# Delta gates moved into the merged mixer stage, with nine attention steps ahead of the first delta head, and two column groups side by side behind a norm

## The chip, the cores and the metric

The kernel runs on one core of a Trainium2 chip. The metric is the device time of one execution in microseconds, the median of several. TensorE (PE in the rows, PEld for its weight loads), VectorE (DVE), ScalarE (ACT), GpSimd (POOL) and the DMA queue that SyncE (SP) issues on each work through their own list of instructions in order. They meet only at semaphores.

## What is computed

Two transformer blocks of two layers each, on 512 tokens of width 1024. The change touches the second block only. Each of its layers does this:

```python
h = rms_norm_2(x, pre_mix_w[l])
u = h @ w_in[l]
(u_conv, dq, dk, dv, gqkv, gz, b_f, b_b, a_f, a_b) = jnp.split(u, offs, axis=-1)
y_conv = conv_module(u_conv, ...)
y_diff = diff_attention(dq, dk, dv, ...)
y_delta = gated_deltanet(gqkv, gz, b_f, b_b, a_f, a_b, ...)
y = jnp.concatenate([y_conv, y_diff, y_delta], axis=-1) @ w_out[l]
x = x + rms_norm_2(y, post_mix_w[l])
h = rms_norm_2(x, pre_mlp_w[l])
y = jnp.square(jax.nn.relu(h @ w_ff1[l])) @ w_ff2[l]
x = x + rms_norm_2(y, post_mlp_w[l])
```

`diff_attention`: six heads; for each block of 128 queries, two softmax maps over 512 keys with a slope times distance, the second subtracted with a factor lambda, then the product with the values. `gated_deltanet`: six heads of width 64, forward and backward. Its gates are `g = -exp(A_log) * softplus(a + dt_bias)` and `beta = sigmoid(b)`; in each chunk a unit lower triangular system is solved, and a state runs from chunk to chunk.

## The kernel before

The layer runs as a sequence of stages. Each has one block of instructions for every engine, and the engines meet at its end.

**Gate stage** (`delta_gates_stage`, L2598). TensorE turns the 24 gate rows (L2615) and six tiles of keys and values to token order (L2620, 24 transposes), then sums the log decays (L2626, L2628). ACT computes the sigmoid, exponentials and logarithm; DVE copies the turned tiles out (L2654).

**Mixer stage** (`mixer_stage`, L2682). It merges the differential attention (24 steps, one for each of six heads and four query blocks) with the delta heads. The delta work of a head stands in seven slots, levels 0 to 6 of the triangular solve; the program counts slots `t = 7 h + level`. In a slot TensorE does `turn(…, 0)` (L2804), `pairs` (L2792 or, at level 0, L2794), `turn(…, 1)`, work of the head before (`before`), an attention piece, `products` (L2812), the preparation of the next head and more of the head before (`behind`), and a second attention piece. ACT copies the turned halves (L2996) and the pairs (L3000); DVE subtracts the products (`update`, L3251), which lets the next level begin. Slots 42 to 48 hold only the states of the last head and the last attention steps.

**An attention step** `s` runs over four to five slots. Lag 0: TensorE's scoring, `scores` (L2899 the slope times distance, L2906 the query-key products). Lag 1: DVE's maximum (`top`, L3190), ACT's exponentials (`exps`, L3019). Lag 2: DVE's inverses, ACT's `rescale` (L3025), DVE's `subtract` (L3204). Lag 3: TensorE turns the first half of the map, ACT copies it (L3031), TensorE turns the second (L2918). Lag 4: ACT copies, TensorE weighs the values (`weigh`, L2925), ACT copies the output (L3036). Steps start every second slot. The scores of all steps share banks 5 and 6, and the numbers come from one line:

```python
s, odd = divmod(t + 2 - lag, 2)
```

Ahead of slot 0 stand the values' transposes (L2942), the first head's preparation (`prepare(0, …)`: two transposed rows of gate sums, L2777, then the key and the query Gram products, L2779) and the scoring of step 0 alone.

**Dense products** (class `Dense`, `run`). Columns are taken in groups of 256. Weights of a unit are split into two halves, high by ACT (L254), low by DVE (L259), in two slots, and TensorE runs low, high by low, high by high (L460 to L462) for each of eight row tiles. Where a `PlainNorm` with `post` goes ahead (`ff1_0`, `in2_1`, `ff1_1`), it first scales the last product by its own norm (L1247), adds it to the stream (L1251 on DVE, L1266 on GpSimd for tiles 1, 3, 5), splits the new stream tile (L1214 on ACT, L1230 on DVE), squares it (L1219), and TensorE sums the squares (L1008) behind each tile of group 0. ACT and DVE split the weights of group 1 when the norm is through. The second norm's factor is spread (L1016) behind tile 3 of group 1, DVE copies it (L1164), and the results are multiplied by it at evacuation (L688, or L675 in `in2_1`).

## Time and profile before

| what | value |
|---|---|
| median of 3 runs | 4175.57 us (4174.79 to 4177.26) |
| the profiled execution | 4178.55 us, span 4176.8 us |
| granted TensorE clock, mean | 0.944 of full |
| PE busy / DVE / ACT / POOL | 3872.8 / 2183.3 / 1495.6 / 344.1 us |
| gates, layers 0 and 1 | from 2418 and from 3381 us |
| `ff1_0`, `in2_1`, `ff1_1` norms | from 2802, 3191 and 3765 us |

All times inside the trace are from the span's start. A granted clock of 0.50 is 1.2 GHz, 1.00 is 2.4 GHz. In rows that list instructions in order of time, "x8" is eight of a kind merged, and the bracket is the idle time of the engine just before and what ended it. A matmul in float32 stands as two passes in the trace, so `weigh` has eight.

### The profile page before, as it was taken

What the parts mean: (1) busy time and instruction counts of PE and PEld (TensorE: products, weight loads), DVE (VectorE), ACT (ScalarE), POOL (GpSimd) and SP (SyncE); (2) the same over time, 40 slices, a digit from 0 to 9 for tenths busy, and PEclk for the clock granted to TensorE, in tenths of its full rate; (3) what the DMA queues carried; (4) which work ended last, traced back from release to release, by engine and by line L of the source; (5) the groups of instructions that cost most, each with busy time, mean ns of one, the idle gap of its engine ahead of it and who ended that gap; (6) DMA issues with size and microseconds to landing.
All of it is one profiled execution on the core that took longest, in us unless ns stands there. A gap on an engine that the chain in (4) does not pass through costs nothing. (4 is left out here: it accounts for less than half of the span.)

```text
span 4176.8 us, 49727 instructions
## 1 busy us (share of the span) xinstructions
PE 3872.8 (93%) x20585; PEld 3106.2 (74%) x20585; DVE 2183.3 (52%) x3124; ACT 1495.6 (36%) x2290; POOL 344.1 (8%) x296
## 2 busy tenths in 40 slices
PE   7997789999999999899999979989998979988998
PEld 4884667888888777678877757757786757866876
DVE  5625765555564332373256746543475846544375
ACT  2115632111453112152255335433364335533264
POOL 0000220000000000000000034200000025400000
PEclk9998889999999999999999979989999979989998
DMA  5500013343222111122322100022231200012231
GB/s 202 174 31 10 6 41 101 111 141 111 66 66 74 58 58 51 38 91 91 100 83 94 61 11 1 1 71 81 90 101 61 87 11 1 1 61 71 91 101 60
DMA packets 254720, 288.90 MB, mean 69 GB/s; under 512 B 6756, under 2 KB 226939, under 8 KB 254517
## 3 DMA queue, kind: packets, MB, share of 16 engines
q1 hardware_dynamic: 252437, 281.84, 20.8%
q10 hardware_dynamic: 2080, 4.19, 0.3%
q8 instruction: 146, 2.39, 0.2%
q14 instruction: 57, 0.47, 0.0%
HBM read 283.92 MB, written 2.10 MB: 68 GB/s over the span
## 5 line engine op out<-in xcount | busy, mean ns | idle before, releaser
L460 PE MATMUL banks<-h_halves,w_halves 128*128 128x512 f32 x3824 | 1435.4, 375 | 83.1 <-DVE h_halves L259 42.3
L461 PE MATMUL banks<-h_halves,w_halves 128*128 128x512 f32 x3824 | 1427.5, 373 | 0.0
L462 PE MATMUL banks<-h_halves,w_halves 128*128 128x512 f32 x3824 | 1420.8, 372 | 0.0
L460 PEld LDWEIGHTS banks<-h_halves,w_halves 128*128 128x128 f32 x3824 | 733.6, 192 | 233.1 <-issue 84.2
L462 PEld LDWEIGHTS banks<-h_halves,w_halves 128*128 128x128 f32 x3824 | 731.0, 191 | 128.0
L461 PEld LDWEIGHTS banks<-h_halves,w_halves 128*128 128x128 f32 x3824 | 733.5, 192 | 121.1 <-issue 0.5
L259 DVE TENSOR_TENSOR w_halves<-work,w_halves 128x2048 fp32r<-128x2048 f32 (+1 forms) x215 | 488.4, 2271 | 469.3 <-ACT w_halves L254 469.1
L254 ACT ACTIVATE w_halves<-work 128x2048 fp32r<-128x2048 f32 (+1 forms) x215 | 407.4, 1895 | 533.7 <-PE banks L462 399.6
L254 ACT ACTIVATE h_halves<-kept 128x512 fp32r<-128x512 f32 (+1 forms) x520 | 333.0, 667 | 313.8 <-PE banks L462 234.4
L259 DVE TENSOR_TENSOR h_halves<-kept,h_halves 128x512 fp32r<-128x512 f32 (+1 forms) x520 | 361.3, 738 | 138.6 <-ACT h_halves L254 137.9
L952 DVE SCALAR_TENSOR_TENSOR kept<-kept 128x512 f32<-128x512 f32 x280 | 188.3, 748 | 7.1 <-DMA kept<-in_mod_w 7.1
L694 ACT ACTIVATE kept<-kept 128x512 f32<-128x512 f32 x64 | 37.4, 633 | 253.8 <-DVE kept L688 253.8
L2119 PE MATMUL banks<-h_halves,w_halves 128*128 128x512 f32 x320 | 121.4, 379 | 3.7 <-DVE h_halves L1116 3.7
L2120 PE MATMUL banks<-h_halves,w_halves 128*128 128x512 f32 x320 | 118.9, 372 | 0.0
L2121 PE MATMUL banks<-h_halves,w_halves 128*128 128x512 f32 x320 | 118.4, 370 | 0.0
L709 ACT ACTIVATE kept<-banks 128x512 f32<-128x512 f32 x66 | 30.0, 529 | 245.9 <-PE banks L462 245.9
L3119 POOL TENSOR_TENSOR work<-work 128x512 f32<-128x512 f32 x84 | 108.9, 1301 | 70.2 <-PE banks L2792 52.4
L3251 DVE TENSOR_TENSOR work<-work,banks 128x512 f32<-128x512 f32 x84 | 62.5, 745 | 94.6 <-PE banks L2812 94.6
L688 DVE SCALAR_TENSOR_TENSOR kept<-banks,kept 128x512 f32<-128x512 f32 x64 | 41.2, 686 | 135.4 <-PE banks L462 135.3
L2135 PE MATMUL banks<-w_halves,h_halves 128*128 128x256 f32 x384 | 108.7, 283 | 0.0
L2134 PE MATMUL banks<-w_halves,h_halves 128*128 128x256 f32 x384 | 108.7, 283 | 0.0
L2133 PE MATMUL banks<-w_halves,h_halves 128*128 128x256 f32 x384 | 108.7, 283 | 0.0
(366 smaller groups left out, 4576.7 us busy)
## 6 DMA issues: line engine op xcount, KB each, us to landing
work<-in_w_ff SPq DMA_DIRECT2D x64, 1024.0 KB, 5.3
work<-in_ffn_w_in SPq DMA_DIRECT2D x44, 1024.0 KB, 5.1
kept<-in_mod_w SPq DMA_DIRECT2D x40, 1024.0 KB, 5.2
work<-in_odd_w_in SPq DMA_DIRECT2D x24, 1024.0 KB, 5.2
work<-in_w_in SPq DMA_DIRECT2D x24, 1024.0 KB, 5.0
work<-in_ffn_w_out SPq DMA_DIRECT2D x16, 1024.0 KB, 5.2
work<-in_even_w_in SPq DMA_DIRECT2D x13, 1024.0 KB, 5.1
work<-in_odd_w_out SPq DMA_DIRECT2D x8, 1024.0 KB, 5.4
```

Source lines behind the costliest of these rows:

```text
L254: return core.nc.scalar.activation(dst, src, ACT.Copy)
L259: return core.nc.vector.tensor_tensor(dst, src, high.bitcast(F32), ALU.subtract)
L460: nc.tensor.matmul(o, low[:, k - a, fc], rh[:, tc], start=(k == 0), stop=False)
L461: nc.tensor.matmul(o, high[:, k - a, fc], rl[:, tc], start=False, stop=False)
L462: mm = nc.tensor.matmul(o, high[:, k - a, fc], rh[:, tc], start=False, stop=(k == K - 1))
L952: ins = nc.vector.scalar_tensor_tensor(out=self.sum(q, n), in0=self.slot(m)[:, k], scalar=c, in1=self.sum(q, n), op0=ALU.mult, op1=ALU.add)
L2119: nc.tensor.matmul(o, low[:, c, fc], rh, start=(c == 0), stop=False)
L2120: nc.tensor.matmul(o, high[:, c, fc], rl, start=False, stop=False)
L2121: mm = nc.tensor.matmul(o, high[:, c, fc], rh, start=False, stop=(c == KD - 1))
L2133: nc.tensor.matmul(o, core.h(c, 1)[:, tc], high[:, c, :], start=(c == 0), stop=False)
L2134: nc.tensor.matmul(o, core.h(c)[:, tc], low[:, c, :], start=False, stop=False)
L3119: nc.gpsimd.tensor_tensor(c4(pl.level[m % 3]), c4(pl.s[h % 2]), mat(pl.pairs[:, cc(lv)]), ALU.mult).then_inc(level_masked, 1)
```

## The change

**Gates in the mixer stage.** `delta_gates_stage` is gone. Its transposes, sums and activations are spread over the head of `mixer_stage`: gate rows into bank 2, token tiles alternately into banks 3 and 4. The loads are issued in another order: gate rows and the distance table first, the level masks (`pairs`) last.

**Nine attention steps ahead of slot 0.** Ten iterations, numbered -10 to -1, run before the level loop (called iterations 0 to 9 below). Steps 0 to 8 start in them, one each in iterations 0 to 8, with their scores alternately in banks 5, 6 and 0, 1. Token transposes stand in iterations 0 to 2, the four preparations of head 0 in iterations 3 to 6. The other 15 steps start 2.75 slots apart. Within a slot the weighing now stands ahead of the turn.

```diff
-    score_bank = lambda m: core.ps[:, 5 + m, :]
+    score_banks = lambda s: (0, 2) if s < AHEAD and s % 2 else (5, 7)
+    score_bank = lambda s, m: core.ps[:, score_banks(s)[0] + m, :]
...
+    AHEAD, EARLY = 9, 10
...
+    starts = {t: s for s, t in enumerate([s - EARLY for s in range(AHEAD)] +
+                                         [1 + (11 * i + 2) // 4 for i in range(N - AHEAD)])}
+
     def step_at(t, lag):
-
-        s, odd = divmod(t + 2 - lag, 2)
-        return s if odd == 0 and 0 <= s < N else None
+        return starts.get(t - lag)
...
+            for t in range(-EARLY, 0):
+                n = t + EARLY
+                if step_at(t, 4) is not None:
+                    weigh(step_at(t, 4))
+                if step_at(t, 0) is not None:
+                    scores(step_at(t, 0))
+                if n < 3:
+                    if n == 2:
+                        gate_totals()
+                    for b in range(2 * n, 2 * n + 2):
+                        tokens(b)
+                if step_at(t, 3) is not None:
+                    turn_step(step_at(t, 3), 0)
+                if 3 <= n < 7:
+                    prepare(0, n - 3)
+                if step_at(t, 3) is not None:
+                    turn_step(step_at(t, 3), 1)
```

That was TensorE's list; these are ACT's and DVE's:

```diff
+            for t in range(-EARLY, 0):
+                n = t + EARLY
+                if step_at(t, 4) is not None:
+                    copy(step_at(t, 4), 1)
+                if step_at(t, 2) is not None:
+                    rescale(step_at(t, 2))
+                if step_at(t, 4) is not None:
+                    out(step_at(t, 4))
...
+                if 3 <= n < 6:
+                    prepare(0, n - 3)
+                if step_at(t, 1) is not None:
+                    exps(step_at(t, 1))
+                    if step_at(t, 1) in split_at:
+                        split(split_at[step_at(t, 1)])
+                if step_at(t, 3) is not None:
+                    copy(step_at(t, 3), 0)
...
+                if step_at(t, 2) is not None:
+                    invert(step_at(t, 2))
+                if step_at(t, 1) is not None:
+                    top(step_at(t, 1))
...
+                if n in (3, 4):
+                    differences(0, n - 3)
+                    low(0, n - 3)
+                    exponents(0, n - 3)
+                    queries(0, n - 3)
+                if n == 5:
+                    key_gram(0)
+                if n == 6:
+                    query_gram(0)
+                if step_at(t, 2) is not None:
+                    subtract(step_at(t, 2))
```

The pairs of slot 0 wait until all nine early steps have left banks 0 and 1 (`pe.wait_ge(exped, 2 * AHEAD)`).

**Two groups side by side.** Where the norm has `post`, tile `k` of group 0 is followed by tile `k - 2` of group 1. Group 1's weights are split ahead of the norm's tiles, and the second norm's factor is spread behind both groups. The weights of group 2 are then split ahead of the evacuation of group 0.

```diff
                 if before is not None:
-                    second(eng)
+                    second(eng, (lambda: weights(0, 1)) if paired else None)
...
+                    if paired and isinstance(i, int) and i * B * C + u == 0:
+                        weights(i, u + 2)
+                        evacuate(i, u)
...
+                def two_groups():
+                    lag = before.LAG
+                    for k in range(K + lag):
+                        if k < K:
+                            group_tile(0, k)
+                            before.after_tile(pe, 0, k)
+                        if k >= lag:
+                            group_tile(1, k - lag)
+                    before.behind_groups(pe)
```

The order of instructions shows it at three places. TensorE at the start of the gates, before: the gate rows (L2615) and tokens, the gate sums, then the values of the attention (L2942), and one scoring (L2899, L2906) among the preparations (L2777, L2779).

```order
L2615 MATMUL banks<-kept 128x24 x4
L2620 MATMUL banks<-kept 128x128 x24
L2626 MATMUL banks<-work 128x24 x2
L2628 MATMUL banks<-work,kept 128x48
L2603 UNCONDITIONAL_BRANCH
L2761 UNCONDITIONAL_BRANCH
L2942 MATMUL banks<-kept 128x128 x12
L2777 MATMUL banks<-kept,work 128x128 x4
L2899 MATMUL banks<-work 128x512 x2
L2906 MATMUL banks<-p_halves 128x512 x6
```

After, at the same place (L2944 the values, L2881 and L2888 the scoring, L2926 the tokens, L2934 and L2936 the gate sums):

```order
L2940 MATMUL banks<-kept 128x24 x4
L2944 MATMUL banks<-kept 128x128 x12
L2881 MATMUL banks<-work 128x512 x2
L2888 MATMUL banks<-p_halves 128x512 x6
L2926 MATMUL banks<-kept 128x128 x8
```

The first scoring has moved up to directly behind the values; the 24 token transposes stand in three lots of eight behind the first three scorings.

TensorE in iteration 4 of the new order: weighing (L2907), scoring, first turn (L2900), a row preparation (L2755), second turn.

```order
L2907 MATMUL banks<-work,kept 64x128 x4
L2881 MATMUL banks<-work 128x512 x2
L2888 MATMUL banks<-p_halves 128x512 x6
L2900 MATMUL banks<-kept 128x128 x2
L2755 MATMUL banks<-kept,work 128x128 x4
L2900 MATMUL banks<-kept 128x128 x2
```

Before, the second row preparation stood between the first scoring and the Gram products, with no other step in flight.

```order
L2906 MATMUL banks<-p_halves 128x512 x6
L2777 MATMUL banks<-kept,work 128x128 x4
L2779 MATMUL banks<-kept 128x128 x8
L2794 MATMUL banks<-kept,work 128x128 x4
L2899 MATMUL banks<-work 128x512 x2
```

Each row preparation now stands inside an attention iteration, ahead of the turn that ends it.

ACT at the head of a paired norm, before (L1026 loads the root's table, L1021 the root, L1214 the high part of a stream tile, L1219 its square):

```order
L507 UNCONDITIONAL_BRANCH
L1026 ACTIVATE kept<-kept 128x1
L1021 ACTIVATE kept<-banks,kept 4x128
L1214 ACTIVATE h_halves<-stream,kept 128x512
L1219 ACTIVATE stream<-stream 128x2x256
```

and after, with the weights of group 1 (L254) between the root and the first tile:

```order
L545 UNCONDITIONAL_BRANCH
L1064 ACTIVATE kept<-kept 128x1
L1059 ACTIVATE kept<-banks,kept 4x128
L254 ACTIVATE w_halves<-work 128x2048
L1259 ACTIVATE h_halves<-stream,kept 128x512
L1264 ACTIVATE stream<-stream 128x2x256
```

L254 stood behind the norm's last root before.

## Rows read from the trace of the kernel before

**Rows 1.** Stretches: PE, PEld, DVE, ACT, POOL busy (count), granted clock, DMA.

```profile
3395.00:3423.20 28.20, 12.89 (x49) 9.34 (x50) 14.41 (x26) 5.65 (x12) 18.27 (x17) 0.56 0.07 19
...
3503.70:3546.00 42.30, 40.36 (x319) 32.96 (x317) 27.11 (x60) 21.53 (x53) 19.50 (x19) 1.00 0.01 1
3546.00:3586.60 40.60, 38.47 (x305) 32.39 (x305) 24.72 (x57) 22.04 (x54) 18.31 (x17) 1.00 0.00 1
...
3663.90:3697.00 33.10, 27.41 (x137) 17.66 (x136) 10.79 (x34) 13.58 (x33) 0.00 (x0) 0.74 0.11 35
```

**Rows 2.** Instructions in time: start, length in us, engine, line, idle before.

```profile
3380.81 0.39 PE L2615 MATMUL banks<-kept 24*128 24x24 f32 x4 [1.65 <-PEq L415]
...
3402.25 1.47 POOL L3123 CAST work<-kept 128x896 f16<-128x896 f32 x1 [191.56 <-DMA work<-in_diff_lambda_k]
...
3404.36 1.01 PE L2899 MATMUL banks<-work 128*128 128x512 f16 x2 [5.70 <-POOL work L3074]
...
3409.40 2.08 PE L2779 MATMUL banks<-kept 64*128 64x128 f32 x8 [1.41 <-DVE work L3210]
...
3422.86 1.03 PE L2899 MATMUL banks<-work 128*128 128x512 f16 x2 [5.07 <-ACT kept L3019]
3423.82 1.64 PE L2906 MATMUL banks<-p_halves 32*128 32x512 f32 x6
3425.39 1.11 PE L2804 MATMUL banks<-kept,work 128*128 128x128 f32 x4
```

**Rows 3.** DMA view, 3380 to 3402: issues, KB each, median us to landing.

```profile
kept<-tables SPq DMA_DIRECT2D x1, 448.0 KB, 3.1
```

**Rows 4.** Instructions in time: the parts of an attention step.

```profile
3421.35 0.69 ACT L3019 ACTIVATE kept<-banks,kept 128x512 f32<-128x512 f32 x1 [1.75 <-DVE kept L3192]
...
3439.98 0.38 PE L2918 MATMUL banks<-kept 128*128 128x128 f32 x2
...
3444.59 1.09 PE L2925 MATMUL banks<-work,kept 128*64 128x128 f32 x8
...
3447.78 0.60 PE L2899 MATMUL banks<-work 128*128 128x512 f16 x2
3448.32 0.97 PE L2906 MATMUL banks<-p_halves 32*128 32x512 f32 x6
```

**Rows 5.** Groups by line: the level update; busy us, mean ns, idle before.

```profile
L3251 DVE TENSOR_TENSOR work<-work,banks 128x512 f32<-128x512 f32 x84 | 62.5, 745 | 94.6 <-PE banks L2812 94.6
```

**Rows 6.** Instructions in time: the stage's end, after the last level update.

```profile
3664.63 0.66 PE L2835 MATMUL banks<-work 128*128 128x64 f32 x4 [0.56 <-DVE work L3251]
...
3670.88 0.66 PE L2835 MATMUL banks<-work 128*128 128x64 f32 x4 [0.20 <-DVE work L3259]
...
3688.84 1.97 PE L2925 MATMUL banks<-work,kept 128*64 128x128 f32 x8 [0.47 <-ACT work L3031]
...
3691.89 2.19 ACT L1440 ACTIVATE work<-kept 128x512 f32<-128x512 f32 x4 [0.28 <-PEq L2754]
```

**Rows 7.** Instructions in time: norm and first two groups of `ff1_1`.

```profile
3770.49 0.75 DVE L1247 SCALAR_TENSOR_TENSOR kept<-kept,banks 128x512 f32<-128x512 f32 x1 [2.17 <-PE banks L1016]
...
3774.66 0.76 PE L460 MATMUL banks<-h_halves,w_halves 128*128 128x512 f32 x1 [4.21 <-DVE h_halves L1230]
...
3784.19 1.04 PE L1008 MATMUL banks<-stream,kept 128*4 128x128 f32 x8
...
3798.57 2.29 DVE L259 TENSOR_TENSOR w_halves<-work,w_halves 128x2048 fp32r<-128x2048 f32 x1 [0.86 <-ACT w_halves L254]
...
3801.01 0.47 PE L460 MATMUL banks<-h_halves,w_halves 128*128 128x512 f32 x1 [4.67 <-DVE w_halves L259]
...
3809.53 0.69 DVE L1164 COPY kept<-banks 128x512 f32<-128x512 f32 x1 [8.67 <-PE banks L1016]
...
3816.49 0.47 PE L460 MATMUL banks<-h_halves,w_halves 128*128 128x512 f32 x1 [1.41 <-DVE w_halves L259]
```

**Rows 8.** Stretches, columns as in rows 1: 4 us of the tail.

```profile
3672.00:3676.00 4.00, 4.00 (x22) 2.57 (x19) 1.19 (x3) 0.27 (x1) 0.00 (x0) 0.57 0.02 4
```

344 lines of the change are left out of this document (199 added, 145 removed).

## The prediction

> **What bounds the kernel now.** I read the stretches of the second delta layer first (its stage of 317 us occurs once for each of the two layers, and nearly the same). In a stretch of the level loop TensorE is busy 40.36 of 42.30 us with four attention scorings in it, and 38.47 of 40.60 us with three [rows 1]: 1.7 us less time for 1.9 us less work. There TensorE is the bound and a moved attention step gives back its TensorE work. Before and behind that loop it is not. From 3395.0 to 3423.2 it is busy 12.89 us and its granted clock is 0.56, that is, nearly all at 1.2 GHz; behind the last level update it is busy 27.41 of 33.10 us at 0.74 [rows 1]. Then I read the instructions in order of time. The first scoring waits 5.70 us for GpSimd's slope, the second 5.07 us for the first step's exponentials [rows 2]. Last I read the norm ahead of the dense products: TensorE stands 4.67 us before the second group of columns, because ACT and DVE split that group's weights only when the norm is done [rows 7].
>
> **Part 1: gates merged, nine steps ahead of the loop.** My mark is the first turning matmul of level 1, at 3425.4 [rows 2]; in the new order it follows iteration 9 and one slot.
>
> Start. The table behind the scoring takes 3.1 us to land [rows 3]. It is now the third load, issued some 1 us into the stage, and the cast no longer waits for the lambda rows. Cast to scoring took 2.1 us (3402.25 to 3404.36) [rows 2]. With the first transposes of the gates at 3380.8 [rows 2] the first scoring comes at about 3381.9 + 3.3 + 2.4 = 3387.6, against 3404.4. So the gates' own stretch goes.
>
> Prices. At the low clock a scoring is 2.53 us (3422.86 to 3425.39) [rows 2], a weighing 1.97 [rows 6], a turn about 0.65 (twice less its drain: 0.38 at full clock) [rows 4], a preparation of four transposes 1.1 and of a Gram product 2.08 [rows 2]. At the full clock: 1.44 for the scoring (0.60 and 0.97 overlapping), 1.09, 0.38, and half of the others [rows 4]. The exponentials take ACT 1.5 us (3421.35 to the scoring at 3422.86 that waits for them) [rows 2, 4]; the two copies, the rescale and the output copy about 1.7 more.
>
> An iteration is a ring over ACT and TensorE: copy 0.4, weighing 1.1, output copy 0.3, exponentials 1.5, copy 0.4, turn 0.5: 4.2 us at the full clock. At the low clock TensorE sets it: copy 0.4, weighing 1.97, scoring 2.53, turn, copy and turn 1.7: 6.6 us. The three iterations with a row preparation are longer, since ACT reads the prepared rows ahead of its exponentials in program order, and DVE makes its differences ahead of the next subtraction. Walked through with these prices: iterations 0 to 2 (scoring, key and value transposes, gates) 3387.6 to 3402.4; iteration 3, 7.5 us; iteration 4, with weighing, scoring, turn, preparation, then 3.7 us of ACT and a turn in a row, 10.3; iteration 5, 8.2, to 3428.4. In it TensorE has no gap. In the kernel before it had none from 3422.86 on, at the low clock, and by 3439.98 the turns run at full clock [rows 2, 4]. So iterations 6 to 9 run mostly at full clock: 5.2, 5.9 (the query Gram product stands ahead of a subtraction), 4.3, 4.1, to 3448; slot 0 with pairs, weighing and two turns 3.0 to 3.5. The mark comes at about 3451.5: **+26 us** in each layer. Bounds: +15 if the clock is full all the way, +35 if it stays low.
>
> Level loop. Slots 1 to 41 lose 5 scorings, 6 turns in pairs and 4 weighings: 5 x 1.4 + 6 x 0.7 + 4 x 1.0 = 15.2 us. But the steps now stand every 2.75 slots, and eight slots hold no attention at all. A level is a ring: turns, pairs, ACT's copy, products, and DVE's 0.745 us update [rows 5]. Its two holes (some 0.65 us until the copy, an estimate, and 0.8 until the update) are filled today by attention; I count 6 us of holes left open, nearly half of them in head 0 and the rest at levels 6 and 0. Net **-9 us**; bounds -13 and -4. The slots just behind the mark ran at the low clock until about 3430; if half of that goes, **-1**.
>
> Tail. From the first value product at 3664.63 to the next stage's first instruction at 3691.89 [rows 6] the last head's four chunk steps share TensorE with two scorings, three turnings and four weighings. The first chunk step took 6.25 us (3664.63 to 3670.88) with a weighing, a scoring and two turns inside, 3.3 us by the prices above; alone I take 3.5, since part of that work filled its own waits. Three such steps, a last half step of 1.8, and some 3.5 for the output products and the last copy end near 3680.5. One turning and weighing remain and fit in the holes: **-11 us**; bounds -8 and -13.
>
> Per layer 26 - 9 - 1 - 11 = +5; both layers **+10**.
>
> The loads moved on SP's queue (table and gate rows first, pairs last) are hidden: the pairs table is needed only at the first level mask. The merged and renamed semaphores, and the changed places of weighing and output copy within a slot, cost nothing I can see; the row that would cover them is the 2 us of slack that ACT has in each slot. The three slope builds on GpSimd are each three slots ahead of use.
>
> The clock rule. The 4 us around 3674 show TensorE busy 4.00 at a granted 0.57, and the tail as a whole 0.74 at 27.41 busy of 33.10 us [rows 1, 8]: in this kernel short gaps between small matmuls do cost the full clock. The Trainium skill says the same (TensorE: Matmul & The Clock Gate, A second HAM failure mode: psum-queue depth-cycling): short idles between groups make the clock swing between its two levels. By that rule iterations 6 to 9 would not stay at 2.4 GHz; this is the first rival.
>
> **Part 2: first two groups side by side, three norms.** Added ahead of the norm: ACT's 1.9 us and DVE's 2.29 us weight split of group 1 [rows 7]. The first scaling started at 3770.49, 2.1 us behind the row products; now DVE's split ends at 3771.6, so the norm starts 1.1 us later, the first matmul at 3775.75 instead of 3774.66. From there TensorE does not wait: with the row sums it took 2.56 us for each tile of group 0 (the starts of seven such row sums lie 2.56 apart, one is shown, 1.04 long) [rows 7], and the tile of group 1 adds 1.36: 3.92 per pair. Two opening tiles to 3781.1, six pairs to 3804.6, the last row sum, two tiles and the spread to 3809.3. ACT and DVE need 2.2 us for a tile and are hidden. What is late next is the evacuation: the spread of the second norm now stands behind both groups, so DVE's copy, 0.69, and the two evacuations, 1.3, hold up group 2 until 3811.6. It began at 3816.49 [rows 7]: -4.9 us. The input product of the second layer has a side task and no gap of 1.41 us ahead of its group 2 as this one has, so there I take -3.9. Sum 2 x 4.9 + 3.9 = **-13.7 us**. Bounds: -17 if the evacuation is hidden, -9 if tiles wait for each other. The 4.67 us stall goes in full; of the low clock behind it 3 us go too, and 2.3 us come back as the evacuation wait.
>
> **Sum.** 10 - 13.7 = -3.7 us. The profiled execution took 4178.55 us, 3 above the median of the runs, 4175.57; on the median that is **4171.9**.
>
> **Rivals.**
> (a) The clock stays at 1.2 GHz until the level loop. For it: 0.56 over the whole stretch today, and the tail [rows 1, 8]. Against it: TensorE would be 90% busy there, and it rose after such work. Iterations 6 to 9 then take 8.4, 6.6, 6.6 and 5: +9 a layer, +18: **4190**, slower. It decides where iteration 7 takes over 6 us.
> (b) The early steps run tighter: full clock from iteration 3, ring of 4.2 us. +15 instead of +26 in each layer: -22, **4150**. For it: the ring itself allows it. Against it: iterations 3 and 4 leave TensorE idle a third of the time.
> (c) The level loop gives back only 4 us a layer, because with fewer attention pieces DVE's update and ACT's copy bound each slot and the clock dips at the head ends: +10, **4182**. Against it: the two stretches of [rows 1], whose length follows TensorE's work one to one.
> (d) The pairing gives nothing, as group 1's tiles only displace group 0's and the norm gets longer: **4186**. Against it: the stall at 3801 is a wait for weights alone.
>
> **How the numbers follow.** Forecast 0.46, with its own range 4163 to 4179; (a) 0.14, (b) 0.18, (c) 0.12, (d) 0.03, mixtures 0.07. A measurement of this kernel tells about 0.2%, 8.4 us, from no change: faster is under 4167.2, slower over 4183.9. Faster: (b) and the quarter of the forecast's case below 4167, with a share of the mixtures: 0.34. Slower: (a), (d) and what (c) has above 4184: 0.20. Range 4152 to 4191: it takes in (c), (d), (a) and half of (b).
>
> **What would show it.** First scoring some 7 us into the stage; iterations of 7 to 10 us with preparations and 4.2 to 6 without; the first level-1 turn about 71 us into the stage instead of 44.6; head stretches of 38.5 to 40 us; 16 us from the last head's first value product to the next stage; TensorE without a gap through two groups, then a gap near 2.3 us before group 2. Wrong would be: iterations that wait for GpSimd or DVE, or a gap within the paired groups.

## The result, and the profile after

The changed kernel takes 4202.1 us (median of 5 runs, 4197.1 to 4205.4), the kernel before 4177.3 (5 runs beside it, 4174.8 to 4178.7): ratio 1.0058, 95% interval 1.0047 to 1.0068. It is slower by 24.9 us. The prediction said 4171.9, range 4152 to 4191, and gave slower a chance of 0.20: it had the kernel faster, and the time lies 11 us above its range.

I cut both profiled executions (spans 4176.8 and 4203.7 us) at the same instructions: the first transpose of the gate rows, the first matmul of the stage behind the mixer, and the row sums that open each norm.

| stretch | before | after | difference | on record |
|---|---|---|---|---|
| mixer of the first layer | 311.8 | 328.6 | +16.8 | +5 |
| mixer of the second layer | 311.8 | 326.2 | +14.4 | +5 |
| `ff1_0`, norm to the next norm | 389.0 | 386.0 | -3.0 | -4.9 |
| `in2_1`, norm to the second mixer | 189.5 | 189.7 | +0.2 | -3.9 |
| `ff1_1`, norm to the last norm | 387.2 | 384.4 | -2.7 | -4.9 |
| all the rest | | | +1.2 | 0 |
| sum | | | +26.9 | -3.7 |

Inside a mixer (the mark is the first turn of level 1; the tail runs from the last level update to the next stage's first matmul):

| | before | after, first layer | after, second layer | on record |
|---|---|---|---|---|
| first scoring | 23.7 | 6.8 | 7.4 | 6.8 |
| mark | 44.7 | 74.2 (+29.6) | 69.0 (+24.4) | +26 |
| mark to last update | 238.5 | 236.2 (-2.3) | 234.9 (-3.6) | -10 |
| tail | 28.6 | 18.1 (-10.5) | 22.3 (-6.3) | -11 |

The columns of the next fences are those of [rows 1]: time, length, busy time of PE, PEld, DVE, ACT and POOL with counts, granted clock, DMA. A dip is a stretch of the level loop in which the granted clock falls below 1.00. First the kernel before, second layer: gates and preamble up to the first update, heads 0 to 5, tail.

```profile
3380.81:3423.31 42.50, 19.34 (x84) 15.26 (x84) 19.73 (x42) 12.11 (x23) 18.39 (x17) 0.59 0.10 27
3423.31:3461.81 38.50, 35.70 (x248) 28.51 (x246) 25.71 (x42) 21.22 (x52) 19.88 (x19) 0.92 0.00 1
3461.81:3503.81 42.00, 39.87 (x305) 33.84 (x306) 24.77 (x57) 21.38 (x53) 19.61 (x19) 0.96 0.00 1
3503.81:3546.11 42.30, 40.29 (x318) 32.85 (x316) 27.11 (x59) 21.64 (x53) 19.50 (x19) 1.00 0.01 1
3546.11:3586.71 40.60, 38.53 (x305) 32.50 (x306) 24.72 (x56) 21.93 (x54) 18.20 (x17) 1.00 0.00 1
3586.71:3628.41 41.70, 40.65 (x318) 33.19 (x316) 25.47 (x57) 20.70 (x51) 23.04 (x21) 1.00 0.01 2
3628.41:3664.01 35.60, 34.20 (x268) 28.40 (x268) 15.05 (x40) 17.97 (x47) 6.13 (x7) 1.00 0.00 1
3664.01:3691.91 27.90, 22.86 (x129) 16.84 (x128) 10.68 (x34) 9.84 (x27) 0.00 (x0) 0.77 0.00 1
```

The same stretches of the changed kernel, second layer, with heads 0 to 5 all shown:

```profile
3395.05:3460.25 65.20, 47.47 (x223) 29.15 (x223) 40.94 (x83) 35.76 (x86) 16.58 (x15) 0.69 0.06 18
3460.25:3502.65 42.40, 35.49 (x239) 29.86 (x240) 21.22 (x33) 19.66 (x46) 23.22 (x20) 0.88 0.01 1
3502.65:3542.25 39.60, 37.74 (x299) 31.67 (x296) 23.06 (x55) 19.56 (x48) 20.13 (x19) 1.00 0.00 1
3542.25:3585.15 42.90, 38.78 (x292) 32.34 (x292) 24.44 (x53) 17.54 (x42) 21.76 (x21) 0.96 0.00 1
3585.15:3625.15 40.00, 37.37 (x288) 31.92 (x288) 21.31 (x51) 19.69 (x48) 20.00 (x19) 0.96 0.01 1
3625.15:3665.15 40.00, 37.93 (x300) 32.03 (x300) 25.49 (x53) 17.34 (x43) 19.99 (x18) 1.00 0.00 1
3665.15:3698.95 33.80, 31.86 (x248) 26.57 (x248) 12.68 (x35) 15.32 (x39) 6.12 (x7) 1.00 0.00 1
3698.95:3720.57 21.62, 17.03 (x80) 13.85 (x80) 6.03 (x24) 3.53 (x10) 0.00 (x0) 0.59 0.00 1
```

To be seen: in head 0 TensorE has fewer instructions than before (239 against 248) and about the same busy time, 35.49 against 35.70, and the head takes 42.4 us instead of 38.5. Head 2 has 292 matmuls instead of 318 and is busy 38.78 us against 40.29, and it takes 42.9 us instead of 42.3: TensorE idles 4.1 us in it instead of 2.0, and part of it runs at half clock (0.96). Behind head 0 the clock falls in heads 2 and 3, where before it fell in head 1 alone. The tail has 80 instructions instead of 129, at a clock of 0.59 instead of 0.77.

The groups by line show where TensorE waits between the first and the last update of that layer: busy us, mean ns, idle before.

```profile
L2785 PE MATMUL banks<-kept,work 128*128 128x128 f32 x288 | 46.9, 288 | 12.4 <-DVE work L3310 11.1 <-ACT work L3011 1.3
L2793 PE MATMUL banks<-work 128*128 128x128 f32 x288 | 40.8, 284 | 2.6 <-ACT work L3011 2.4
```

The turning matmuls (L2785) wait 12.4 us, nearly all for DVE's update; their counterpart in the kernel before, L2804, waited 6.6 us over the same part of the loop.

### The profile page after: what moved, and what is told of

Read it like the earlier page. It is cut to its first block and busy times, and to the rows that moved or that the text cites. A ratio compares the mean times of both kernels' runs of the same rounds, so it can differ in the third digit from the quotient of the medians.

```text
span 4203.7 us, 49713 instructions
## 1 busy us (share of the span) xinstructions
PE 3901.4 (93%) x20585; PEld 3120.6 (74%) x20585; DVE 2185.4 (52%) x3124; ACT 1498.7 (36%) x2290; POOL 349.5 (8%) x296
## 3 DMA queue, kind: packets, MB, share of 16 engines
q1 hardware_dynamic: 252437, 281.84, 20.7%
## 5 line engine op out<-in xcount | busy, mean ns | idle before, releaser
L465 PE MATMUL banks<-h_halves,w_halves 128*128 128x512 f32 (+1 forms) x3728 | 1393.4, 374 | 60.3 <-DVE h_halves L259 42.5
L466 PE MATMUL banks<-h_halves,w_halves 128*128 128x512 f32 (+1 forms) x3728 | 1388.7, 373 | 0.0
L467 PE MATMUL banks<-h_halves,w_halves 128*128 128x512 f32 (+1 forms) x3728 | 1381.8, 371 | 0.0
L465 PEld LDWEIGHTS banks<-h_halves,w_halves 128*128 128x128 f32 x3728 | 714.6, 192 | 201.2 <-issue 48.8
L467 PEld LDWEIGHTS banks<-h_halves,w_halves 128*128 128x128 f32 x3728 | 712.4, 191 | 123.3
L466 PEld LDWEIGHTS banks<-h_halves,w_halves 128*128 128x128 f32 x3728 | 714.2, 192 | 117.7 <-issue 0.5
L254 ACT ACTIVATE w_halves<-work 128x2048 fp32r<-128x2048 f32 (+1 forms) x215 | 407.3, 1894 | 524.7 <-PE banks L467 388.6
L254 ACT ACTIVATE h_halves<-kept 128x512 fp32r<-128x512 f32 (+1 forms) x520 | 332.5, 666 | 313.5 <-PE banks L467 234.9
L2165 PE MATMUL banks<-h_halves,w_halves 128*128 128x512 f32 x320 | 121.4, 379 | 3.8 <-DVE h_halves L1155 3.8
L2166 PE MATMUL banks<-h_halves,w_halves 128*128 128x512 f32 x320 | 118.9, 372 | 0.0
L2167 PE MATMUL banks<-h_halves,w_halves 128*128 128x512 f32 x320 | 118.5, 370 | 0.0
L2785 PE MATMUL banks<-kept,work 128*128 128x128 f32 x576 | 94.3, 289 | 24.9 <-DVE work L3310 22.2
L2181 PE MATMUL banks<-w_halves,h_halves 128*128 128x256 f32 x384 | 108.7, 283 | 0.0
L2180 PE MATMUL banks<-w_halves,h_halves 128*128 128x256 f32 x384 | 108.7, 283 | 0.0
```

The source lines that it names most:

```text
L254: return core.nc.scalar.activation(dst, src, ACT.Copy)
L465: nc.tensor.matmul(o, low[:, k - a, fc], rh[:, tc], start=(k == 0), stop=False)
L466: nc.tensor.matmul(o, high[:, k - a, fc], rl[:, tc], start=False, stop=False)
L467: mm = nc.tensor.matmul(o, high[:, k - a, fc], rh[:, tc], start=False, stop=(k == K - 1))
L2165: nc.tensor.matmul(o, low[:, c, fc], rh, start=(c == 0), stop=False)
L2166: nc.tensor.matmul(o, high[:, c, fc], rl, start=False, stop=False)
```

## Experiments

All times are medians of the device time; "before" ran beside each batch and had medians of 4173.9 to 4177.3. Mixer figures come from the profiled execution of each kernel.

**1. The pairing alone.** The norms of the change, the mixer of before.

```diff
+    delta_gates_stage(core, nc, a, l, pl)
     mixer_stage(core, nc, a, l, pl)
```

(against the change, with both functions as in the kernel before)

> The kernel before with the three paired norms alone; gates and steps as before. The terms on record give -13.7 us against before. The profile of the changed kernel gives another sum: row sums to row sums, its ff1_0 stretch is 2.97 us shorter, its in2_1 stretch 0.20 longer, its ff1_1 stretch 2.72 shorter, together -5.5 us. Theory 1 (the two parts add up and the pairing was over-priced): -5 to -6, 4172. Theory 2 (the parts work on each other, for example through a clock that the mixer leaves behind): nearer to -13.7, 4164.

Measured: 4168.3 us, ratio 0.9984 (0.9975 to 0.9993), -7.8 us. In the profiled execution the three stretches came out at 386.07, 189.65 and 386.63 us, 3.3 us less than before together. The first mixer, which is not touched, took 308.0 instead of 311.8, and the unchanged stages ahead of the first gates 4.8 us less. So how much of the 7.8 us is the pairing's is known only roughly: 3.3 us by these stretches, 5.5 by those of the change.

**2. Gates and steps alone.** The mixer of the change, the norms of before.

```diff
-        self.paired = post is not None
```

> The kernel before with the merged gates and the nine steps ahead alone; norms unpaired. The terms on record give +10 us. Theory 1 (parts add up): the profile of the changed kernel has +16.8 us in the first mixer and +14.4 in the second, so about +31 to +32, 4209. Theory 2: the parts work on each other, and this part alone costs less, near +10 to +20.

Measured: 4209.6 us, ratio 1.0085 (1.0071 to 1.0098), +33.5 us. With experiment 1 that makes +25.7; the change measured +24.9. The parts add up, the loss is all in the mixer, and the pairing gains about half of its price on record at most.

**3. The earlier spread.**

```diff
-    LAG = 2
+    LAG = 3
...
                             group_tile(1, k - lag)
-                    before.behind_groups(pe)
+                        if k == K:
+                            before.behind_groups(pe)
```

> As the pairing alone, but the second group runs three tiles behind the first instead of two, and the spread of the second norm stands ahead of the last two tiles of group 1, so that DVE can empty the banks while TensorE still works. The 2.11 us that TensorE waited ahead of group 2 should fall to about 0.7 (DVE's weight split ends some 4.6 us behind the last row sums, the copy and two evacuations 2 us later, TensorE arrives at 6.0). Theory A (the lost gain is the low clock that this wait brings): group 2 starts 1.4 us earlier and runs at full clock at once, which is worth another 1.1, 3.0 and 2.2 us at the three sites: -10 to -11 us against the pairing alone. Theory B (the loss behind group 2 is something else): only 3 x 1.4 = -4 us.

Measured: 4157.1 us, ratio 0.9960 (0.9946 to 0.9973), -11.2 against the pairing alone: Theory A. TensorE does not wait at all before group 2.

**4. The gap filled.** Seven matmuls that nobody reads, and nothing else.

```diff
                     before.behind_groups(pe)
+                    for _ in range(7):
+                        nc.tensor.matmul(core.ps[:, 5, 0:P], core.ident(), core.ident(), start=True, stop=True)
```

> As the pairing alone, with seven matmuls of the identity by itself (about 0.28 us each at full clock, into a bank that nobody reads) between the spread and group 2, in the 2.11 us in which TensorE waits there. Nothing else moves. Theory A (the wait lowers the clock and the low clock costs the gain): granted clock 1.00 through group 2 at all three sites, -5 to -6 us against the pairing alone, though group 2 starts no earlier. Theory B (the clock is no cause): no change, or up to +1 us where the filling ends late.

Measured: 4156.0 us, ratio 0.9955 (0.9941 to 0.9968), -12.3 against the pairing alone, in Theory A's sense and twice its size. Here are the 4 us before and the 8 us behind the start of group 2 in `in2_1`, first with the pairing alone:

```profile
3223.57:3227.57 4.00, 1.90 (x12) 1.31 (x10) 3.12 (x5) 3.13 (x2) 0.00 (x0) 0.91 0.44 125
3227.57:3231.57 4.00, 4.00 (x9) 3.14 (x10) 4.00 (x5) 1.29 (x3) 0.00 (x0) 0.50 0.41 142
3231.57:3235.57 4.00, 4.00 (x15) 3.20 (x14) 3.56 (x6) 1.52 (x2) 0.00 (x0) 0.74 0.84 262
```

and with the gap filled, the same three windows, then two instructions there (L509 is the filling, two records for each of the seven):

```profile
3221.39:3225.39 4.00, 3.65 (x26) 2.95 (x25) 3.12 (x5) 3.14 (x2) 0.00 (x0) 1.00 0.43 125
3225.39:3229.39 4.00, 4.00 (x17) 3.30 (x18) 4.00 (x5) 1.29 (x3) 0.00 (x0) 1.00 0.40 137
3229.39:3233.39 4.00, 4.00 (x19) 3.31 (x18) 3.56 (x6) 1.52 (x2) 0.00 (x0) 1.00 0.84 262
```

```profile
3223.21 1.83 PE L509 MATMUL banks<-kept 128*128 128x128 f32 x14
3225.39 0.50 PE L465 MATMUL banks<-h_halves,w_halves 128*128 128x512 f32 x1 [0.35 <-DVE kept L715]
```

Both show the same DVE and ACT work; with the filling TensorE makes 36 matmuls in the 8 us behind the gap instead of 24. That is the clock. The profiled executions are 9.1 us apart: the three stretches are 7.1 us shorter, where Theory A had 5 to 6; 1 us of it lies ahead of group 2 in `in2_1`, where half clock ended sooner. The second mixer is 2.9 us shorter, 308.0 us instead of 310.9 with the same instructions, and that is not the filling's doing as far as anything here shows. The same two lengths occur again and again: 311.8 twice in the kernel before, 310.9 and 308.0 in experiment 1, 307.9 and 307.6 in experiment 3. The loops are alike (240.4 to 240.7 us from first to last update); the tail takes 25.3 or 28.6 us, by its clock. So a single mixer's time in one execution says nothing finer than some 3 us. The play ahead of the first gates is larger: that half of the kernel, with the same 12165 or 12166 TensorE records in each of the sixteen profiled executions, took 2413.0 to 2420.8 us, with 208 to 232 us of it at half clock.

**5. Three steps ahead.**

```diff
-    AHEAD, EARLY = 9, 10
+    AHEAD, EARLY = 3, 7
...
-                                         [1 + (11 * i + 2) // 4 for i in range(N - AHEAD)])}
+                                         [1 + 2 * i for i in range(N - AHEAD)])}
```

> Gates merged as in the change, norms unpaired, but only three steps ahead (in seven iterations) and the other 21 steps two slots apart from slot 1. Theory M (what costs is each step put ahead of the loop, since it is paid there at half clock): iterations 3 to 6 carry no scoring, so the first level-1 turn comes about 44 us into the stage, as before; the loop has as many scorings as before; the tail loses the last two steps, 6 to 8 us. Together -12 to -16 us against the kernel before: 4162. Theory P (the gates and the row preparation through ACT, DVE and GpSimd set the time of the first level, whatever attention runs beside them): the mark stays near 60 us, +15 a layer, -7 in the tail: about +15, 4191.

Measured: 4159.0 us, ratio 0.9960 (0.9948 to 0.9973): Theory M. Marks at 45.8 and 47.8 us, tails 20.5 and 20.7.

**6. Five steps ahead.** As experiment 5 with `AHEAD = 5` and `1 + (13 * i + 3) // 6`.

> As e4_three_ahead with five steps ahead in seven iterations, the other 19 spaced 13/6 slots. Theory M: two more scorings and turnings in iterations 3 to 6 at the low clock, mark at 50 to 55 us, the loop gives back 2 to 3 us, the tail is as in e4: about 0 to +4 us against before, 4178, that is 12 to 18 us over e4. Theory P: no later than e4_three_ahead, and 2 to 3 us less a layer.

Measured: 4161.0 us, ratio 0.9966 (0.9954 to 0.9977), only 2 us over three ahead; the intervals overlap. Marks at 53.4 and 56.3 (7.6 and 8.5 later), loops of 233.9 and 234.0 from first to last update, tails of 18.7 and 19.0. The mark moved much as M says (50 to 55 on record), the total did not (M had 12 to 18 us over three ahead). The first update came only 5.2 and 6.1 us later. The loop of the second layer had a large dip with three steps ahead (head 2 took 43.6 us at 0.92, the whole loop 238.3) and with five only the small one in head 4 (41.6 us at 0.96) that both layers have. The tails shortened by 1.8 and 1.7.

**7. One step ahead.** `AHEAD, EARLY = 1, 7`, the others at `2 * i`: the merging of the gates by itself.

> Gates merged as in the change, norms unpaired, one step ahead in seven iterations, the other 23 two slots apart from slot 0: the loop and the tail are those of the kernel before. It measures the merging of the gates alone. Theory M (the merged stage starts its first scoring 17 us earlier and the row preparation follows in 16 to 20 us): first level-1 turn at 36 to 39 us instead of 44.6, -6 to -9 a layer, 4160 to 4165, no better than three ahead, whose two further steps it leaves in the tail. Theory P (a preparation through ACT, DVE and GpSimd of its own length): mark as before, 4177.

Measured: 4163.1 us, ratio 0.9974 (0.9965 to 0.9984). Marks at 37.2 and 37.6 us (7.4 and 7.0 earlier), loop and tail as before.

**8. The preamble filled.**

```diff
+            def warm(n):
+                for _ in range(n):
+                    nc.tensor.matmul(core.ps[:, 3, :], pl.dist16[:, 0:P], pl.dist16[:, 0:SEQ], start=True, stop=True)
...
                 if step_at(t, 3) is not None:
+                    warm(6 if n < 5 else 3)
                     turn_step(step_at(t, 3), 1)
```

> Gates and nine steps ahead as in the change, norms unpaired, with idle matmuls from iteration 3 on (128x512 f16, about 0.21 us at full clock, into a bank that nobody reads): six ahead of iteration 3, six or three ahead of each second turning, two ahead of each weighing, so that TensorE has no gap there. Theory C (iterations 3 to 9 are long because TensorE runs at half clock, and it does so because of its gaps): granted clock 1.00 from about iteration 4 on, iterations of 5 us, first level-1 turn at 55 to 58 us instead of 69 to 74, -12 to -16 a layer against the unfilled form: about 4182. Theory R (the ring over ACT and DVE sets the iterations, or the clock does not answer to the filling): no gain, or +3 to +8 a layer, since the filling then takes its time at half clock.

Measured: 4191.3 us, ratio 1.0040 (1.0026 to 1.0054), -18.3 against experiment 2: Theory C, at two thirds of its size (marks at 60.6 and 64.6 us, not 55 to 58). Preamble of the first layer, in the changed kernel to its first update, and with the filling (its first three iterations, then iteration 3 to the first update):

```profile
2417.97:2488.79 70.82, 52.42 (x223) 32.05 (x224) 39.92 (x83) 36.77 (x86) 15.99 (x16) 0.61 0.06 17
```

```profile
2417.20:2440.00 22.80, 15.68 (x89) 9.65 (x90) 16.03 (x37) 12.71 (x26) 6.75 (x8) 0.78 0.18 50
2440.00:2475.20 35.20, 30.78 (x182) 17.13 (x180) 24.28 (x48) 22.96 (x61) 9.16 (x9) 1.00 0.00 1
```

The first update comes 58.0 us into the stage instead of 70.8 (67.9 in experiment 2), though TensorE does more, and 61.9 us in the second layer instead of 65.2. Without the filling the same 223 matmuls took 62.7 to 73.9 us in ten preambles (the change, experiments 2, 9, 10 and 11), at granted clocks of 0.76 down to 0.53, so both filled ones lie below all of them. They still come 15.4 and 19.5 us later than in the kernel before: with the clock at 1.00 a step ahead costs less, and it still costs.

The Trainium skill (TensorE: Matmul & The Clock Gate, Part 4: PE-mode transpose) has it that the full clock does not engage for transposes. Where transposes are mixed with other matmuls the trace does not bear that out: the row above is a stretch of many transposes with other matmuls among them at a granted 1.00, and two turning transposes that take 0.69 us at half clock take 0.44 at full (rows of L2900 further below); no run here has transposes alone.

**9. The bare slots filled.** Twelve 128x128 f16 matmuls ahead of `turn(h, lv, 0)` in 22 slots, behind a wait for the exponentials of the last step begun.

> Gates and nine steps ahead as in the change, norms unpaired, with twelve small idle matmuls (128x128 f16) at the start of each of the 22 slots of the level loop that have neither scoring nor turning behind the slot before; bank 5, whose scores have been read. Nothing in the preamble. Theory C (a third of the lost gain of the loop is clock: dips that follow bare slots): no dips in the loop, its length from the first to the last update 4 to 5 us shorter in each layer: -8 to -10 us against the unfilled form. Theory R (bare slots are bound by the ring turn, copy, products, update at some 4.6 us, and filling only lengthens them): 0 to +6 us.

Measured: 4210.4 us, ratio 1.0091 (1.0069 to 1.0113), no gain, as Theory R has it. Behind head 0 the dips go but for one, in head 3, and the loop becomes longer, 244.4 us in both layers (233.9 and 239.0 in experiment 2). What kept the total was 4 us less in each tail and an earlier first update in the first layer (62.7 us), neither of them touched by the edit. Heads 2 and 3 of the first layer:

```profile
2558.90:2601.00 42.10, 39.45 (x333) 33.11 (x330) 23.74 (x52) 17.31 (x41) 21.49 (x21) 1.00 0.01 1
2601.00:2643.20 42.20, 40.32 (x346) 34.98 (x347) 21.17 (x51) 19.91 (x48) 19.61 (x19) 0.96 0.00 1
```

**10. The weighing one slot later.**

```diff
+    weigh_at = {start_of(n) + (5 if AHEAD <= n < N - 1 and start_of(n + 1) - start_of(n) > 2 else 4): n for n in range(N)}
...
-                    for s, work in ((step_at(t, 4), weigh), (step_at(t, 3), lambda s: turn_step(s, 0))):
+                    for s, work in ((weigh_at.get(t), weigh), (step_at(t, 3), lambda s: turn_step(s, 0))):
```

> Gates and nine steps ahead as in the change, norms unpaired; in the level loop a step whose successor stands three slots on is weighed in its sixth slot instead of its fifth (and its output copied there). Same work, no filling. In the change the attention of three slots falls as turning | scoring, turning and weighing | nothing, and these take 5.2 to 6.8, 7.1 and 4.7 us; here it falls as turning | scoring and turning | weighing. Theory L (the loop gave back too little because the work is bunched: a full slot is TensorE's, a bare one the ring's 4.6 us): some 0.8 us in each of ten periods, and fewer dips of the clock: -6 to -10 us a layer, 4190 to 4197 against 4209.6 for the unfilled form. Theory S (the length is the sum of work and the ring's holes wherever the pieces stand): within 3 us of 4209.6.

Measured: 4199.6 us, ratio 1.0057 (1.0040 to 1.0073), -10 against experiment 2, and yet not for the reason of Theory L. The slots did even out (5.3, 6.3 and 6.2 us where there had been 5.3, 7.1 and 6.3), but the loop of the first layer took 233.8 us against 233.9, with two dips (heads 3 and 5, both at about 0.95) where experiment 2 had none behind head 0. The gain is 3.0 and 3.8 us in the tails and 1.8 us in the loop of the second layer.

**11. The loop without attention, and 12. with six steps fewer.** The first leaves out steps 9 to 23, the second has three steps ahead, the next fifteen at the slots of the change, and leaves out the last six (`[:18]`).

```diff
-    steps = [(h, i) for h in range(6) for i in range(4)]
+    steps = [(h, i) for h in range(6) for i in range(4)][:9]
```

> Gates and nine steps ahead as in the change, norms unpaired; the fifteen attention steps of the level loop and tail are left out (their outputs are not computed). It measures the level loop without attention. Theory F (a bare slot is a ring of turn, copy, products and update with its own floor, 4.6 to 4.8 us, 2.2 at level 0 and some 6.8 at level 6): 195 to 200 us from the first to the last update at full clock, more where the clock falls, since TensorE is idle a quarter of the time: up to 210. Fifteen steps then cost the loop 34 to 39 us, 2.3 to 2.6 each, not the 3.3 of their TensorE work. Theory W (the loop's length is TensorE's work plus 11 us of holes, as in the kernel before): 234 - 15 x 3.3 = 185 us. With the tail at 16 us, about 4209.6 - 2 x 42 = 4126 by F, 4105 by W.

> Three steps ahead in seven iterations, norms unpaired, and the next fifteen steps at the places that the loop of the change has for its fifteen (slots 1, 3, 6, 9, 12, ...); the last six steps are left out. Against e4_three_ahead (20 scorings in the loop, 234 us at full clock) it takes out five more scorings and their turnings and weighings without putting them into the preamble. Theory F (bare slots have a floor): 226 to 229 us from the first to the last update, that is 1.0 to 1.6 us for a step. Theory W: 234 - 5 x 3.3 = 217 us. Where the loop comes out at 226 to 229 while the change needs 234 to 239 for the same fifteen, the difference is what the leftovers of the early steps and the half clock behind them cost in head 0 and what dips cost.

Measured: 4156.6 and 4153.2 us. The bare loop takes 214.1 and 212.9 us from the first to the last update, even more than Theory F's upper bound of 210; the loop of the second takes 232.3 and 231.2, where F had 226 to 229. Both are far from Theory W (185 and 217), and both contain dips. The bare loop, first layer, heads 0 to 2:

```profile
2478.40:2514.10 35.70, 29.45 (x208) 25.57 (x208) 15.06 (x22) 13.48 (x31) 21.61 (x19) 0.90 0.00 0
2514.10:2548.80 34.70, 29.68 (x240) 26.52 (x240) 17.11 (x40) 10.85 (x24) 19.52 (x19) 1.00 0.00 1
2548.80:2586.70 37.90, 32.81 (x240) 29.32 (x240) 17.54 (x40) 11.30 (x24) 19.86 (x19) 0.91 0.00 1
```

Heads 1 and 2 have the same 240 matmuls. At a clock of 1.00 a head without any attention takes 34.7 us, at 0.91 it takes 37.9. Outside level 0 (2.2 us) no bare slot at full clock takes less than 4.5 us, and many take 5 to 6.3. A head of the changed kernel with two or three steps takes 39.5 to 44.2. Heads 1 to 5 of the first layer as one stretch, in experiment 5 (three ahead), experiment 2 (nine ahead) and experiment 12, whose attention there is that of experiment 2:

```profile
2495.80:2694.44 198.64, 191.51 (x1516) 158.79 (x1515) 117.49 (x264) 102.08 (x253) 89.25 (x83) 1.00 0.01 1
2523.42:2716.79 193.37, 180.70 (x1426) 151.97 (x1424) 106.75 (x240) 89.42 (x216) 87.87 (x81) 1.00 0.00 1
2497.59:2695.12 197.53, 184.72 (x1426) 155.83 (x1424) 108.38 (x241) 90.75 (x218) 89.43 (x82) 0.97 0.00 1
```

The first two are free of dips, the third has three (heads 2 to 4). By the first two, 10.8 us less work for TensorE give 5.3 us less time.

**13. Both halves mended.** Three steps ahead with experiment 3.

> Three steps ahead (e4) and the paired norms with the earlier spread (e3) in one kernel. If the two parts only add up: -17.6 and -19.0 us, 4140. If part of what e3 brought was a luckier clock in the mixer, which e4 has in its own way: 4143 to 4150.

Measured: 4139.7 us, ratio 0.9912 (0.9896 to 0.9929). They add up (4140 on record).

**14. And filled.** Experiment 13, with experiment 8's filling in its seven iterations and this ahead of the paired groups:

```diff
                     before.tensor(pe)
                     if paired:
+                        for _ in range(8):
+                            nc.tensor.matmul(core.ps[:, 5, 0:P], core.ident(), core.ident(), start=True, stop=True)
```

> As e11_three_ahead_paired, with idle matmuls at two places where TensorE waits at half clock: eight of the identity by itself (0.56 us each at half clock) in the 5.1 us ahead of a paired norm's first tile, and those of e7 in iterations 3 to 6. Theory C (the clock follows how steadily TensorE is kept busy): the full clock comes 3 to 4 us sooner in the paired groups, -1.5 to -2 us at each of three sites, and the first level-1 turn comes 4 to 6 us earlier in each layer: -12 to -18 us against e11, some 4125. Rival (filling at half clock delays as much as it gives back): 4138 to 4144.

Measured: 4123.3 us (4120.5 to 4127.4), ratio 0.9876 (0.9860 to 0.9893): 16.5 us below experiment 13, 51 us below the kernel before beside it and some 79 below the change. The three paired stretches are 7.8 us shorter than in experiment 13 together, the mixers 3.4 and 0.5 (the second had a tail mostly at half clock, 25.5 us against 20.9). Another 4.1 us of the 18.0 between the two profiled executions lie in the unchanged stages ahead of the first gates, so the filling's own share is nearer to 12 us by its stages than to 16.5.

## Why the prediction was wrong, point by point

**The preamble: right.** First scoring at 6.8 and 7.4 us into the stage (6.8 on record), mark at +29.6 and +24.4 (+26). The walk through the ring held in its parts. Iterations 4 and 7 of the second layer, the first with a row preparation, the second without one:

```profile
3425.93 1.03 PE L2881 MATMUL banks<-work 128*128 128x512 f16 x2
...
3432.81 0.69 PE L2900 MATMUL banks<-kept 128*128 128x128 f32 x2 [2.80 <-ACT work L3046]
3433.98 1.97 PE L2907 MATMUL banks<-work,kept 128*64 128x128 f32 x8 [0.47 <-ACT work L3046]
...
3446.76 0.60 PE L2881 MATMUL banks<-work 128*128 128x512 f16 x2
...
3449.42 0.44 PE L2900 MATMUL banks<-kept 128*128 128x128 f32 x2 [0.80 <-ACT work L3046]
3450.33 1.97 PE L2907 MATMUL banks<-work,kept 128*64 128x128 f32 x8 [0.47 <-ACT work L3046]
```

The first is ten us long (scoring to scoring 3425.93 to 3435.88), all at half clock, with the predicted long wait for ACT; the second is 5.5. The clock did roughly what the forecast said in the second layer (full from within iteration 5, 3436.6, to the end of iteration 7, 3450.2, where the weighing takes 1.97 again, and once more from 3453.6 to 3460.5), and what rival (a) said in the first, where the full clock of iterations 1 and 2 was lost in iteration 3 and, but for 4 us, did not come back before the loop. So (a)'s mechanism was there, in one layer of two, worth 5 us. That both marks came so near to +26 is in part luck: the same preamble put its mark at 66.5 to 77.3 us over the ten executions named in experiment 8. Rival (b), the tight ring, was not: iterations 3 and 4 left TensorE idle a third of the time, as the argument against it had it.

**The level loop: the step that failed.** The record has "Level loop. Slots 1 to 41 lose 5 scorings, 6 turns in pairs and 4 weighings ... = 15.2 us", then 6 us of holes and 1 us of clock: -10. It was -2.3 and -3.6. The argument stood on two stretches of [rows 1], heads 2 and 3, 1.7 us less time for 1.9 us less work. The next head of the same trace does not follow it: from head 3 to head 4 the work grows by 2.1 us (38.53 to 40.65) and the time by 1.1 (40.6 to 41.7). From first to last update, by scorings whose work lies inside the loop:

| kernel | scorings | first layer | second layer |
|---|---|---|---|
| before | 21 | 240.7 | 240.7 |
| three ahead (experiment 5) | 20 | 234.0 | 238.3 |
| five ahead (6) | 19 | 233.9 | 234.0 |
| nine ahead (2) | 15 | 233.9 | 239.0 |
| the change | 15 | 239.7 | 238.7 |
| fifteen, clean head 0 (12) | 15 | 232.3 | 231.2 |
| none (11) | 0 | 214.1 | 212.9 |

These lengths hold dips, and different ones: behind head 0 only 234.0 (three ahead) and 233.9 (nine ahead), both first layers, are free of them. The dip-free heads 1 to 5 of experiment 2 (193.4 us) with the clean head 0 of experiment 12 (34.8 us in its first layer) would make about 228 us, an estimate, within Theory F's 226 to 229. So from 20 scorings to 15 the loop gives back about 6 us, for 5 x 3.3 = 16 us of TensorE work at my prices. The holes of a slot (turn, wait for ACT's copy, products, wait for DVE's update) grow as the work goes. Three pieces can be told apart, by heads; the record's terms for heads 1 to 5, counted out slot by slot, are 13 us of work and 3 of holes, -10, and for head 0 about 0:

- work and holes at full clock. Heads 1 to 5 took 202.2 us before, with a dip in head 1 (42.0 us at 0.96; it took 40.4 at 1.00 in experiment 1), so 200.6 without it. In the first layer of experiment 2 they take 193.4: -7.2 where the record had -10;
- dips. The same head 2, with the same 292 matmuls, takes 41.3 us at a clock of 1.00 in experiment 2, 44.2 at 0.92 in the first layer of the change. Heads 1 to 5 of the change lie 5.7 and 2.9 us above the dip-free 193.4, against 1.6 before: +4.1 and +1.3. The record had nothing for this;
- head 0. The record had "nearly half" of the 6 us of holes there. In experiment 12, where no early step is left over, head 0 takes 34.8 and 36.5 us; in the change 40.6 and 42.4, against 38.5 before. The leftovers of the early steps, partly at half clock, cost about 6 us. From the mark to head 1 the change is 0.8 and 2.3 us slower than before.

The three make -2.3 and -3.6. In the first layer the largest miss is the clock; in both, the work moved out is worth less than one to one. Where no dip fell behind head 0 (first layer of experiment 2) the same instructions gave back 8.0 us from the mark on.

```profile
2562.90:2604.20 41.30, 37.23 (x292) 31.11 (x292) 24.25 (x52) 17.39 (x42) 21.67 (x21) 1.00 0.00 1
```

```profile
2568.87:2613.07 44.20, 40.18 (x292) 33.90 (x292) 24.06 (x52) 17.55 (x42) 21.61 (x21) 0.92 0.00 1
```

The first row is experiment 2, the second the change. Rival (c) named this mechanism, "with fewer attention pieces DVE's update and ACT's copy bound each slot and the clock dips at the head ends", and priced it at 4 us given back. I gave it 0.12, and the argument against it was the slope of two stretches. A third stretch, and a bound from the other side (what a slot takes when nothing is left in it), were missing. That the dips come from the holes is argued, not shown: the filling of experiment 9 removed most of them, and it changed the slots as well.

**The tail: right where the clock held.** -10.5 in the first layer (-11 on record), -6.3 in the second, where the tail ran at 0.59. Experiment 2 had the short gain in both layers, 22.1 and 22.6 us, at 0.58 and 0.57. [rows 8] had shown that the tail falls to half clock; the sum did not carry it over to a tail with less work in it.

**The pairing: mechanism right, size wrong.** The stall of 4.67 us went; the first matmul came 0.9 us later behind the first spread (1.1 on record); pairs took 3.93 us (3.92); the wait ahead of group 2 was 2.11 us (2.3). Group 2 started 4.1, 2.8 and 4.9 us earlier (4.9, 3.9, 4.9 on record). Then 1.1, 3.0 and 2.2 us were lost behind it, because the 2.11 us brought the half clock for the next 3.4 to 6.8 us, which the 1.41 us of the kernel before [rows 7] had not. The record has "2.3 us come back as the evacuation wait", which is the wait without the clock behind it. Experiments 3 and 4 show it: without the wait, or with the wait filled, the clock stays at 1.00, and the three stretches are 10.9 and 7.1 us shorter than in experiment 1. The Trainium skill (TensorE: Matmul & The Clock Gate, HAM oscillation — how this bites in real kernels) has it that DMA waits of 3 to 5 us between bursts of matmuls make the next burst start cold. Here a wait of 2.11 us, shorter than those, already did, and one of 1.41 us did not. The forecast also took the pairs at full clock from the start: behind the longer wait of 5.10 us the half clock lasted 6.0, 5.7 and 3.6 us, where it had lasted 3.2 to 3.5.

```profile
2829.80 0.77 PE L491 MATMUL banks<-h_halves,w_halves 128*128 128x512 f32 x1 [5.10 <-DVE h_halves L1275]
2867.11 0.79 PE L465 MATMUL banks<-h_halves,w_halves 128*128 128x512 f32 x1 [2.11 <-DVE kept L726]
```

These two, of `ff1_0`, answer to the second and the last row of [rows 7]. Rival (d) is out: the stretches of the change are 5.5 us shorter, and pairing alone gains 7.8 us by the medians.

**The sum.** On record +10 and -13.7; measured +33.5 and -7.8, each by itself. In rival (a) the four iterations add up to 26.6 us, 7.1 over the forecast's 19.5; where the other 2 of its 9 us come from is not said. Between the sum on record and the profiled execution lie 30.6 us: 14 are the level loop, 8 the pairing, 5 the tail of one layer, 2 the preambles (3.6 over in one layer, 1.6 under in the other), 1 the rest.

Three of these misses are one omission: the half clock behind gaps that the change opens or moves, in the loop, in the tail and ahead of group 2, stood in the sum at nothing.

Open: why the clock fell in the loops, preambles and tails in some executions and not in others with the same instructions, and whether experiment 10's shorter tails are more than that play. Nor was it tried to split experiment 14's gain between its two fillings, other than by the stretches.

## What to carry to other kernels

A slope read between two stretches is not a rule: read all stretches of the trace, and before work is moved out of a loop, ask what an iteration takes with nothing in it. Here half to two thirds of TensorE's work came back, not all of it. Each gap that a change opens or moves on TensorE is to be priced with the half clock behind it, and a few matmuls into a bank that nobody reads, or an earlier release of the banks, can be worth more than the gap. Moving work ahead of a loop pays for as much as fits into waits that are there anyway (here three to five steps, not nine). When two profiled executions are compared, look first at the stages that are the same in both: here they differ by up to 8 us.

## What the runs showed of the hardware that I had not expected

Filling 2.11 us of waiting with idle matmuls at three places took 12.3 us off the median, 7.1 of them seen in the three stretches, though the waits for DVE ended no earlier for it. A gap of 1.41 us ahead of group 2 left the clock at full, one of 2.11 us halved it, at all its sites (two of the one, three of the other). The same instructions come out at different clocks from execution to execution: the same mixer took 310.9 to 311.8 or 307.6 to 308.0 us, the same preamble 62.7 to 73.9, the same first half of the kernel 2413.0 to 2420.8. The kernel before spreads over 4166 to 4181 us in all batches; that this play makes up the spread is likely and not shown. And filling is no remedy everywhere: in the loop's bare slots it held the clock behind head 0 but for one dip, and made heads 1 to 5 each 0.8 to 3.4 us longer than the dip-free ones of experiment 2. That it did so because it stood ahead of a turn that could otherwise have started is argued, not shown.
